# Delta rule inside a hybrid block: the first level of the triangular inverse as a transpose and two subtractions

## The reference, cut to what matters

```
N = where(strict, (kb @ k.T) * Lmask, 0)     # 64 x 64, strictly lower triangular
A = N + eye(C)
sol = triangular_solve(A, [vb, kb * exp(gc)], lower=True)
u, w = sol[:dk], sol[dk:]
Aqk = (q @ k.T) * Lmask
# scan over the chunks
v_new = u - w @ state
o = q_e @ state + Aqk @ v_new
state = state * d + k_e.T @ v_new
```

## Time and profile before

| | us |
|---|---|
| median of 3 runs | 3423.39 |
| lowest and highest of them | 3422.58, 3426.14 |
| the profiled execution, first to last instruction (span) | 3420.3 |
| TensorE matmul busy in the span | 3348.4 (98%) |
| VectorE busy | 2278.8 (67%) |
| ScalarE busy | 1593.4 (47%) |
| GpSimd busy | 339.6 (10%) |
| the delta rule's stretch | about 2826.8 to 2966.9 |

### The profile page before, as it was taken

How to read it: one execution, slowest core, us unless ns; L and a number is a source line. 1 busy time by engine, 2 the same in 40 slices (tenths; PEclk the granted TensorE clock), 3 DMA queues, 4 the chain that set the end, 5 groups by cost and what they waited for, 6 DMA issues and landing times. The chain is left out here.

```text
span 3420.3 us, 48737 instructions
## 1 busy us (share of the span) xinstructions
PE 3348.4 (98%) x18576; PEld 2856.2 (84%) x18576; DVE 2278.8 (67%) x3709; ACT 1593.4 (47%) x2932; POOL 339.6 (10%) x375
## 2 busy tenths in 40 slices
PE   8999999999999999999999999999999999999999
PEld 7998888877788899887887888888787888889987
DVE  6887474778447787853565576667465567678865
ACT  3565254454433455555324363346355243355654
POOL 1000200022010100022010100000000104222200
PEclk9999999999999999999999999999999999999999
DMA  6346312220334435520454242245410330142464
GB/s 218 109 149 206 111 49 64 91 69 25 104 102 137 157 108 170 173 73 25 160 161 143 75 134 97 96 165 168 122 38 26 109 99 26 38 148 81 136 200 157
DMA packets 107988, 386.48 MB, mean 113 GB/s; under 512 B 12060, under 2 KB 14764, under 8 KB 107504
## 3 DMA queue, kind: packets, MB, share of 16 engines
q1 hardware_dynamic: 101088, 364.86, 32.6%
q0 software_dynamic: 4528, 16.43, 1.5%
q10 hardware_dynamic: 2144, 2.10, 0.2%
HBM read 379.13 MB, written 4.21 MB: 112 GB/s over the span
## 5 line engine op out<-in xcount | busy, mean ns | idle before, releaser
L445 DVE TENSOR_TENSOR w_low<-ring,w_high 128x1024 fp32r<-128x1024 f32 (+1 forms) x481 | 591.3, 1231 | 496.3 <-ACT w_high L433 490.6
L433 ACT ACTIVATE w_high<-ring 128x1024 fp32r<-128x1024 f32 (+1 forms) x481 | 485.0, 1010 | 491.8 <-PE bank L469 212.8
L469 PE MATMUL bank<-x_low,w_high 128*128 128x512 f32 (+1 forms) x1712 | 654.9, 388 | 19.5 <-DVE w_low L445 13.0
L469 PE MATMUL bank<-x_high,w_low 128*128 128x512 f32 (+1 forms) x1712 | 641.4, 380 | 0.0
L469 PE MATMUL bank<-x_high,w_high 128*128 128x512 f32 (+1 forms) x1712 | 417.8, 381 | 0.0
L469 PEld LDWEIGHTS bank<-x_low,w_high 128*128 128x128 f32 x1712 | 323.1, 189 | 82.4 <-issue 17.6
L469 PEld LDWEIGHTS bank<-x_high,w_low 128*128 128x128 f32 x1712 | 323.4, 189 | 56.9 <-issue 3.6
L469 PEld LDWEIGHTS bank<-x_high,w_high 128*128 128x128 f32 x1712 | 304.6, 189 | 59.1 <-issue 4.8
L738 PE MATMUL bank<-w_low,x_high 128*128 128x512 f32 (+1 forms) x384 | 145.6, 379 | 3.6 <-ACT z_z L2102 1.5
L740 PE MATMUL bank<-w_high,x_high 128*128 128x512 f32 (+1 forms) x384 | 143.5, 374 | 0.0
L739 PE MATMUL bank<-w_high,x_low 128*128 128x512 f32 (+1 forms) x384 | 143.5, 374 | 0.0
(11 more groups left out here) (821 smaller groups left out, 8215.0 us busy)
## 6 DMA issues: line engine op xcount, KB each, us to landing
ring<-in_W SPq DMA_DIRECT2D x686, 512.0 KB, 3.5
X<-in_x POOLq DMA_DIRECT2D x1, 2048.0 KB, 9.7
x_spill<-X POOLq DMA_DIRECT2D x1, 2048.0 KB, 8.2
X<-x_spill POOLq DMA_DIRECT2D x4, 512.0 KB, 3.5
ring<-in_W SPq DMA_DIRECT2D x4, 432.0 KB, 4.0
out<-X SPq DMA_DIRECT2D x3, 512.0 KB, 5.5
const<-in_consts POOLq DMA_DIRECT2D x1, 1133.0 KB, 10.6
f_hid<-in_xT ACTq DMA_DIRECT2D x4, 256.0 KB, 8.2
```

The source lines that it names most:

```text
L433: ac.activation(b.UH[u.place][:, 0:u.K * u.n], u.src(), ACT.Copy).then_inc(*b.split.act.up("high", i))
L445: dv.tensor_tensor(b.UL[u.place][:, 0:n], u.src(), b.UH[u.place][:, 0:n].bitcast(F32), SUB).then_inc(*b.split.dve.up("low", i))
L469: i = pe.matmul(out, w[:, k, c], v, start=n == 0 and q == 0, stop=last and q == 3 * K - 1)
```

## The change

Level 0 starts from the identity in both tiles, so its result is known without a product: the inverse so far is the identity minus the masked matrix, and the other tile is the identity minus its transpose. The change does this: TensorE transposes `d_nm` into a bank (two transposes), VectorE computes `d_y` = identity - `d_nm` and `d_xi` = identity - bank. The three products of level 0, ScalarE's copy of the first and the two copies of the identity go. Level 0 takes one step (10) instead of two, so each later step of the chunk is one earlier, `LEAD3` is 16 and `STEPS3` 27, and there are 75 steps. GpSimd masks level 1 in step 10, and waits for the subtraction `d_y` first, since it overwrites `d_nm`, which that subtraction reads.

```diff
 tensor_delta
-    for l in range(6):
+    yield
+    bank = b.bank(("t", 0, c, w), g.dve.at("x", 0, c, w))
+    for e in bank.emptied:
+        pe.wait_ge(*e)
+    pe.wait_ge(*g.pool.at("level", 0, c, w))
+    turned(bank.ap[:, 0:256].rearrange("p (h c) -> p h c", h=2), pair(s.NM, w)).then_inc(*g.pe.up("t", 0, c, w))
+    for l in range(1, 6):
         yield
         pe.wait_ge(*g.pool.at("level", l, c, w))
-        pe.wait_ge(*(g.dve.at("x", l - 1, c, w) if l else g.dve.at("one", c, w)))
+        pe.wait_ge(*g.dve.at("x", l - 1, c, w))
 scalar_delta
-    for l in range(6):
+    yield
+    for l in range(1, 6):
 vector_delta
-    if c:
-        dv.wait_ge(*g.pe.at("u", c - 1, w))
-    dv.tensor_copy(P(s.XI), bc(b.ident, 1, 2)).then_inc(*f.up())
-    dv.tensor_copy(P(s.Y), bc(b.ident, 1, 2)).then_inc(*f.up("one", c, w))
...
-    for l in range(6):
+    yield
+    dv.wait_ge(*g.pool.at("level", 0, c, w))
+    if c:
+        dv.wait_ge(*g.pe.at("u", c - 1, w))
+    dv.tensor_tensor(P(s.Y), bc(b.ident, 1, 2), P(s.NM), SUB).then_inc(*f.up("y", 0, c, w))
+    dv.wait_ge(*g.pe.at("t", 0, c, w))
+    dv.tensor_tensor(P(s.XI), bc(b.ident, 1, 2), got("t", 0), SUB).then_inc(*f.up("x", 0, c, w))
+    for l in range(1, 6):
 gpsimd_delta
+        if l == 1:
+            gp.wait_ge(*g.dve.at("y", 0, c, w))
         gp.tensor_tensor(P(s.NM), P(s.NT), bc(lev[:, l, :], 1, 2), MUL).then_inc(*f.up("level", l, c, w))
...
         yield
-        yield
+        if l:
+            yield
-STEPS3 = 23 + REST3
-LEAD3 = 17
+STEPS3 = 22 + REST3
+LEAD3 = 16
```

More of the change, by code:

```diff
@@ L3986, in tensor_delta @@
         pe.wait_ge(*g.act.at("t", l, c, w))
+        pe.wait_ge(*g.dve.at("y", l - 1, c, w))
         if l < 5:
-            pe.wait_ge(*(g.dve.at("y", l - 1, c, w) if l else g.dve.at("one", c, w)))
             heads(("x", l), s.Y, s.T1, g.dve.at("x", l, c, w))
-        else:
-            pe.wait_ge(*g.dve.at("y", l - 1, c, w))
         heads(("y", l), s.T1, s.Y, g.dve.at("y", l, c, w))
@@ L4107, in vector_delta @@
     dv.tensor_tensor(P(s.AQ), got("a"), P(s.E), MUL).then_inc(*f.up("a", c, w))
-    for l in range(6):
+    yield
[6 more added lines that the diff above has]
+    for l in range(1, 6):
         yield
         yield
[L4111 to L4114, removed]
+        dv.wait_ge(*f.at("x" if l == 1 else "y", l - 1, c, w))
         if l < 5:
```

## The result

| | before | with the change |
|---|---|---|
| median of 20 runs each, us | 3425.18 | 3429.37 |
| lowest, highest | 3421.57, 3428.12 | 3423.83, 3438.93 |
| span of the profiled execution | 3420.3 | 3425.0 |

The ratio of the times is 1.0015, with a 95% interval of 1.0009 to 1.0022. The kernel became slower by 0.15%, and the interval leaves out "no change". The forecast was 3424.1 us and no change. 3429.37 lies inside the range (3418.5 to 3429.5), at its upper end, but that is luck: the kernel moved the other way than "no change", and the reason for it is not among the rivals.

What follows compares the result with a forecast made beforehand. TensorE, busy 98% of the span, was taken to set the pace. Gains of 2.6 us and losses of 3.3 gave net 0.7 us slower than the median 3423.39, so 3424.1 us, range 3418.5 to 3429.5.

Steps and rivals of the forecast that it cites:

- The copies of the identity: VectorE's copies removed: 0.81 us sooner at the entry, 0.52 us gained in step 7 of each of chunks 1 to 3.
- The entry: Chunk 0: level 1's products x and y begin 1.44 us earlier; with one filler less, a gain of 1.1 us.
- The chain at level 1: Mask, subtraction `d_y`, next mask delay level 1's product t in chunks 1 to 3: loss 0.24 us each, 0.7 in all.
- Contention: Level 1: VectorE's second `d_y` running beside GpSimd's two masks adds 0.31 us to them.
- `w_low`: VectorE's moved conversion delays the subtractions or masks: losses of 1.3, 0.95 and 0.3 us in chunks 1 to 3, sum 2.55.
- the four fillers owed in the last: Four fillers move behind the chunks, at 0.32 us each, so places reached with one filler less gain 0.32 less.
- The sum of these: Whole kernel: gains 2.6 us, losses 3.3 us, net 0.7 us slower.
- What would show it: Level 1: TensorE waits for `d_nm` about 12 us together; stage length about the same, three fillers at its end.
- I am wrong if: Signs against the forecast: level 1's product t follows the second filler at once, or masks there take over 1.5 us each.
- Rival 3: Level 1 of each chunk: VectorE's subtractions and GpSimd's masks hold each other off, 7.8 us in all, 3431.9 us; chance 0.06.
- Rival 2: GpSimd and VectorE early enough everywhere, so TensorE's removed work counts in full: gain 11.1 us, 3412.3 us; chance 0.08.
- What can be measured: Whole kernel: a measurement can tell about 0.2% (6.8 us) from no change, so no measurable change was forecast.

Runs made afterwards that it cites:

- x4: Kernel before, with level 0 reading the constant identity in place of VectorE's copies of it; one execution, 3429.45 us, stage 137.68 us.
- x1: Changed kernel plus useless identity products on TensorE (7, then 6) ahead of level 1's product t in every chunk; 3426.88 us, ratio 1.0004.
- x5: Changed kernel with level 1's mask written to `d_t`, older chunk's outputs a step earlier, `d_xi` before `d_y`, conversions a step later; 3413.09 us, ratio 0.9965.
- x7: Changed kernel plus the useless identity products ahead of level 1's product t in chunk 3 only; one execution, 3428.64 us, stage 145.53 us.
- x8: Kernel before, with GpSimd making level 1's mask three times more than needed in chunks 1 to 3; one execution, 3444.52 us, stage 159.17 us.
- x2: Changed kernel with level 1's mask written into the free `d_t`, so GpSimd need not wait for `d_y`; 3422.43 us, ratio 0.9994.
- x3: Changed kernel with each `w_low` conversion on VectorE one step earlier; one execution, 3429.56 us, stage 142.20 us.
- x6: Changed kernel with only the older chunk's outputs `d_o` one step earlier on VectorE; one execution, 3427.09 us, stage 142.48 us.
- x9: Changed kernel with four extra fillers per later chunk moved from steps 5 to 8 to step 11, ahead of level 1's product t; 3422.04 us, ratio 0.9992.
- a0_change: The changed kernel without any edit, run once more; 3430.61 us, ratio 1.0013 against the kernel before.

## Why the prediction was right and wrong, step by step

- **The copies of the identity.** Forecast 0.81 at the entry and 0.52 in each step 7. x4 shows 1.40 for the first two together, then 0.50 and 0.49. Right. In the changed kernel the state's products start without a wait (2859.81, `d_state,d_t`), against the earlier trace rows.
- **The entry.** Forecast x and y 3.8 us after the transposes, measured 3.84 (2833.75 to 2837.59). The transposes start 0.11 later from R0 than forecast. R0 to R1 is 1.96 shorter, and 1.44 + 0.52 is 1.96. Right.
- **The chain at level 1.** Forecast in chunk 3 from R: first mask from 1.8, product t at 2.6 and 4.25. The rows:

```profile
2940.85 0.48 PE L469 MATMUL bank<-x_high,w_low 128*128 128x512 f32 x1
...
2942.14 0.41 DVE L4113 TENSOR_TENSOR d_y<-const,d_nm 128x256 f32<-128x256 f32 x1
...
2942.69 0.73 POOL L4172 TENSOR_TENSOR d_nm<-d_nT,const 128x256 f32<-128x256 f32 x1 [2.42 <-DVE d_y L4113]
2942.80 0.90 DVE L4113 TENSOR_TENSOR d_y<-const,d_nm 128x256 f32<-128x256 f32 x1
2943.38 0.91 POOL L4175 TENSOR_TENSOR d_aq<-d_aq,const 128x256 f32<-128x256 f32 x1
2943.47 0.71 PE L3955 MATMUL bank<-d_xi,d_nm 128*128 128x128 f32 x4 [0.86 <-POOL d_nm L4172]
```

  `d_y` at R + 1.29 (forecast 1.30), the mask at 1.84, product t at 2.62, and in the second pair at 4.17. x and y were forecast at R + 5.0 and came at 5.53 (2946.38). The missing 0.5 is no wait: the second product t and the filler behind it already run at half clock.
- **Contention.** Forecast 0.31 for a product beside two masks, from the earlier trace rows. Here `d_y` takes 0.90 beside a mask of 0.73, and `d_aq` behind it 0.91, which is 0.2 longer than the next mask of its kind. The Trainium skill (SBUF — State Buffer, "SBUF: two separate sides") has the two exclude each other for a whole instruction. The trace does not quite agree: `d_y` would then end its full 0.42 behind the mask's end and push `d_aq` by as much, but it ends 0.28 behind it (2943.70 for 2943.42), and `d_aq` is 0.2 longer.
- **`w_low`.** Forecast 1.3, 0.95 and 0.3. From x1 with its overrun taken off, the cuts from R1 on are about 34.7, 34.7 and 29.8; by the forecast (before, -0.08 for the chain, -0.52 for step 7 in the first two, the conversion, and the four fillers owed in the last) they would be 35.1, 34.7 and 30.1. The first and the third were 0.3 to 0.4 too high.
- **The sum of these.** Forecast a net loss of 0.7; the stage at full clock is about 140.0 for 140.1, a difference of -0.1. By this estimate every term of the sum held within 0.4 us.
- **The step that failed.** "Then the stretches of the delta rule: ... the granted clock is 1.00 (the 2.4 GHz level) in both." I took the clock as given, and priced every wait at its own length. The sum has no term for what a wait does to the products behind it, and no rival says it. I had even forecast waits of 12 us in places where the trace had only 0.81, and three of four chunks pay for theirs with TensorE at half speed: 6.9 us in the profiled execution. It is shown by filling the waits (x1: no dip, and by the mean clock of 11 executions no more time at half clock than before), by breaking the chain (x5), by removing the dip of one chunk and no other (x7), and by making dips in a kernel that had none in this stage (x8). x2, x3, x6 and x9 agree, within what single profiled executions can show. The Trainium skill (TensorE: Matmul & The Clock Gate, "A second HAM failure mode: psum-queue depth-cycling") says that short idle times between groups of matmuls make the clock swing between its two levels. The trace agrees, in another setting and with waits for a mask: 17.07 us at the lower level in a stage of 146.90. The 0.4 us for each us of dip is from the runs.
- **What would show it.** Waits for `d_nm` were to be about 12 us and are 8.2. Three things lie between: the trace counts a wait from the modelled end of the record ahead (counted from starts, as the forecast does, the eight waits come to 9.7); in each later chunk TensorE has already waited 0.4 at the second transposes for the output `d_o` (1.2 in all), which the forecast left out; and in chunk 1 the first product t, at half clock, takes 0.4 out of the second wait. "Three fillers at its end" is what stands there (2971.55, `x_high,w_high` x3). "I am wrong if ... the masks there take over 1.5 us each": they take 0.73, so this sign would have found nothing. I looked for engines that hold each other off, and the slower side came from the bounding engine itself.
- **The rivals.** Rival 3 (slower) got the sign by a mechanism that did not occur: its price was 1.96 a chunk in the masks. Rival 2 named 11.1 us; x5 gets 8.6 us of stage, 6.2 of it from TensorE's work of 8.8, so most of that work was real and the chain was what held it back.
- **What can be measured.** "About 0.2% (6.8 us)" was too coarse: 20 runs of each kernel tell 0.15% from no change (interval 1.0009 to 1.0022). The forecast time also stood on 3423.39, the median of 3 runs, where 20 give 3425.18; measured against that the kernel is 4.2 us slower for a forecast of 0.7.

The stage of the profiled executions is 6.8 us longer (and 6.9 in a0_change), while the medians differ by 4.2 us (20 runs each), and by 5.3 beside a0_change (4.5 by the ratio). The mean clocks account for most of this: the profiled execution of the kernel before spent 7.0 us at half clock and its 27 executions beside a0_change 19.3 on average, while the change has 29.3 in the profiled one and 31.2 on average over its 20. So the typical difference is some 12 us at half clock and not 22, which is an estimated 5 us of time at 0.4 for each. In which stages the other executions have their dips, and what decides whether a given wait brings one, stays open.

## What to carry to other kernels

Work that is taken from the bounding engine at a place where the next step hangs on a chain of other engines turns into waiting, and the waiting may cost more than its length, here where the granted clock fell with it: look at the granted clock behind each new wait, and give "the clock falls here" a rival of its own. Work out the chain first; then break it (write to a free tile, let ready work of older chunks go ahead; x5 is 8.6 us under the kernel before in the stage and 12 in the median) or put work that is due anyway into the wait (x9, 9.9 us under the change in the stage, but not shown to be faster than the kernel before).

## What the runs showed of the hardware that was not expected

- What stood ahead of a dip: a wait of 0.39 and one of 1.99 us (change, chunk 1; 6.83 us at level 0.50), of 0.39, 0.86 and the first 0.8 of 1.82 (chunk 2; 6.83), of 0.40, 0.86 and 0.83 (chunk 3; 3.41), of 0.40, 2.16 and 0.40 (x2, chunk 1; 3.41). None followed 0.49, 0.86 and 0.84 (x3, chunk 1), 0.65 and 0.61 (chunk 0 of the change) or 0.40, 1.06 and 0.84 with five fillers between the first two (x9, chunk 1). So the length of the longest wait does not decide it, and near waits of 0.8 us the same row of waits can go either way.
- The clock can fall on either side of the wait's end: 0.1 us behind it (change, chunks 1 and 3), 1.4 us behind it (x8, chunk 1), or 1.0 and 2.1 us before it, with TensorE idle (change, chunk 2; x8, chunk 3).
- All dips in these executions are 3.41 or 6.83 us long, those of the last stage aside, and some stand outside the delta rule in programs that are the same there: one near 1915 us in every profiled execution (3.41 or 6.83), one near 1087 in 9 of 12, others between 2372 and 2487 in some, one at 2634 in x2. The start of the stage varies from 2825.42 to 2837.77, more than this change is worth. Dips do not account for all of that: the change as timed has 10.24 us of them ahead of the stage and starts at 2825.42, a0_change, the same program, has 13.65 and starts 4.65 later.
- A filler behind another filler starts 0.23 us later (2907.75 to 2907.98), where one between products stands at 0.32.
